# Mixture-of-experts kernel: GpSimd's gate multiplication as tensor-tensor with a repeated column

## What is computed

```python
top_v, top_i = lax.top_k(logits, TOP_K)          # TOP_K = 2 of 8 experts
gates = jax.nn.softmax(top_v, axis=-1)
...
for e in range(N_EXPERTS):
    out = out + combine[..., e:e + 1] * swiglu(h, w1[e], w3[e], w2[e])
```

## Time and profile before

| what | value |
|---|---|
| runs shown | 1646.36, 1650.67, 1651.36 us, median 1650.67 |
| span of the profiled execution, first to last instruction | 1645.5 us |
| TensorE busy in the span | 96% |
| DVE busy | 78% |
| ACT busy | 63% |
| GpSimd busy | 9% |
| mean granted TensorE clock | 0.990 |
| HBM traffic | 278 GB/s over the span |

### The profile page before, as it was taken

The page is one execution under the profiler, slowest core; times in us unless marked ns, Lnnn a source line. Parts: engine busy times, 40 slices in busy tenths (PEclk is TensorE's granted clock), DMA queues, the critical chain, the costliest instruction groups (busy, mean ns, idle before and its releaser), DMA issues.

```text
span 1645.5 us, 27766 instructions
## 1 busy us (share of the span) xinstructions
PE 1585.1 (96%) x10290; PEld 1363.3 (83%) x10290; DVE 1283.7 (78%) x1252; ACT 1041.8 (63%) x1038; POOL 139.9 (9%) x152
## 2 busy tenths in 40 slices
PE   7999989999899999899999999999999999999997
PEld 7987789999898778788888888888888888888776
DVE  4885556555558656688889889889888888988997
ACT  4634454344354445577777777777777777777675
POOL 1062000000006200100000000000000000001720
PEclk9999999999999999999999999999999999999999
DMA  7429165542252105699999999999999999999992
GB/s 252 159 89 398 55 256 184 186 170 99 80 176 88 40 2 225 247 374 375 382 375 374 389 375 377 382 374 384 378 375 361 399 373 367 395 373 369 398 356 111
DMA packets 68272, 457.56 MB, mean 278 GB/s; under 512 B 7296, under 2 KB 8480, under 8 KB 16752
## 3 DMA queue, kind: packets, MB, share of 16 engines
q1 hardware_dynamic: 59984, 425.80, 67.1%
q0 software_dynamic: 8080, 30.84, 4.9%
q10 hardware_dynamic: 144, 0.05, 0.0%
HBM read 433.07 MB, written 23.59 MB: 278 GB/s over the span
## 4 chain that ended last, share of the span: by engine, by line
PE 54%; issue 3%; DVE 3%; ACT 2%; DVEq 0%; ACTq 0%
PE bank L417 33%; PE bank L442 17%; DVE wl L495 2%; PE bank L430 1%; ACT wh L491 1%; PE bank L738 1%; PE bank L1271 1%; DVE gl L586 0%; PE bank L814 0%; PE bank L1276 0%; PE bank L483 0%; DVE gate L577 0%; ACT wide L1770 0%; ACT oh L728 0%; DVE rstd L2026 0%
## 5 line engine op out<-in xcount | busy, mean ns | idle before, releaser
L495 DVE TENSOR_TENSOR wl<-ring,wh 128x2048 fp32r<-128x2048 f32 x369 | 854.0, 2318 | 157.7 <-ACT wh L491 154.4
L491 ACT ACTIVATE wh<-ring 128x2048 fp32r<-128x2048 f32 x369 | 706.6, 1917 | 99.5 <-PE bank L442 46.9
L417 PE MATMUL bank<-wh,xh 128*128 128x512 f32 x896 | 358.0, 400 | 3.6 <-DVE wl L495 3.0
L417 PE MATMUL bank<-wh,xl 128*128 128x512 f32 x896 | 350.3, 391 | 0.0
L417 PE MATMUL bank<-wl,xh 128*128 128x512 f32 x896 | 349.6, 390 | 0.0
L417 PEld LDWEIGHTS bank<-wh,xh 128*128 128x128 f32 x896 | 168.3, 188 | 36.7 <-DVE wl L495 3.7
L417 PEld LDWEIGHTS bank<-wh,xl 128*128 128x128 f32 x896 | 168.2, 188 | 35.5
L417 PEld LDWEIGHTS bank<-wl,xh 128*128 128x128 f32 x896 | 168.7, 188 | 32.2
L442 PE MATMUL bank<-wh,gh 128*128 128x512 f32 x448 | 175.4, 392 | 6.3 <-DVE gl L586 6.3
L442 PE MATMUL bank<-wh,gl 128*128 128x512 f32 x448 | 174.4, 389 | 0.0
L442 PE MATMUL bank<-wl,gh 128*128 128x512 f32 x448 | 174.3, 389 | 0.0
(11 more groups left out here) (336 smaller groups left out, 2434.2 us busy)
## 6 DMA issues: line engine op xcount, KB each, us to landing
ring<-in_moe_w SPq DMA_DIRECT2D x336, 1024.0 KB, 5.0
ring<-in_ffn_w SPq DMA_DIRECT2D x33, 1024.0 KB, 4.8
ring<-in_w_in SPq DMA_DIRECT2D x24, 1024.0 KB, 4.9
ring<-in_w_out SPq DMA_DIRECT2D x8, 1024.0 KB, 4.8
job_x<-xrow POOLq DMA_DIRECT2D x1, 8192.0 KB, 27.3
job_y<-xrow POOLq DMA_DIRECT2D x1, 8192.0 KB, 47.7
xrow<-job_x POOLq DMA_DIRECT2D x7, 512.0 KB, 9.3
job_y<-yj POOLq DMA_DIRECT2D x7, 512.0 KB, 4.4
```

The lines of the kernel that those rows point to most:

```text
L417: ins = nc.tensor.matmul(up_bank(run, par, 0)[:], x[:, 0:C], w[b][:, k], **kw)
L491: nc.scalar.activation(wh[:, buf], flat_slot(slot), ACT.Copy).then_inc(sem("w_high"), 1)
L495: nc.vector.tensor_tensor(wl[:, buf], flat_slot(run.place(i)[0]), wh[:, buf].bitcast(F32), ALU.subtract).then_inc(sem("w_split"), 1)
```

## The change

The multiplication by one scalar per partition becomes a multiplication of two tensors, the second of which is the same gate column, repeated along the row by a step of zero. Shapes, order, waits and the additions behind it stay.

```diff
             for tt in range(TT):
                 for i in range(2):
                     y = yrow(tt, i)
-                    settle(nc.gpsimd.tensor_scalar(y, y, choice("gate")[:, i, tt:tt + 1], None, ALU.mult))
+                    settle(nc.gpsimd.tensor_tensor(y, y, choice("gate")[:, i, tt:tt + 1].broadcast_to([P, D]), ALU.mult))
                     settle(nc.gpsimd.tensor_tensor(xtok()[:, tt], xtok()[:, tt], y, ALU.add), "rows_summed")
```

## The result

The changed kernel takes 1654.7 us (median of 6 runs, 1651.3 to 1659.2), the kernel before 1647.5 beside it (median of 6, the three that were shown among them, 1646.0 to 1651.4): ratio 1.0038, 95% interval 1.0024 to 1.0052, some 6.3 us slower (4.0 to 8.6). Forecast were +7.7 us and 1658.4, range 1651 to 1662.

What follows compares the result with a forecast made beforehand. DVE was taken to bound the stretch of GpSimd's sums, TensorE the rest. Delays of 17.4 us, less 3 x 1.1 made good and 0.6 cushion, lose 13.4 against 5.7: +7.7 us, 1650.67 to 1658.4, range 1651 to 1662.

Steps and rivals of the forecast that it cites:

- So it gets in even between back-to-back subtractions.: DVE's paired subtractions: a queued GpSimd tensor-tensor starts between them too, giving three places in each DVE step.
- first rival: Last job's sums: a queued tensor-tensor gets in only at `gl` and `gate`, not inside the pair; +5.7 us, 1656.4; chance 0.19.
- A repeated operand costs the same, and I take 2.59 us.: GpSimd's new products of 128x1024: each priced like an addition with two full operands, 2.59 us.
- the 0.628 us: Duration of 256-wide GpSimd instructions with a repeated operand, used as evidence that repetition saves nothing against 0.61 us.
- The third rival: GpSimd's products: the repeated operand is fetched once, 1.06 us each; +1.7 us, 1652.4; chance 0.10.
- Delay 2.42: Inside DVE's subtraction pair: each queued GpSimd tensor-tensor delays the next `wl` by 2.42 us, at three places.
- 2.09: At `gl` and `gate` on DVE: each queued GpSimd tensor-tensor delays the next `wl` by 2.09 us, at four places.
- 17.4: DVE beside GpSimd's eight instructions: total delay in us, 1.77 + 3 x 2.42 + 4 x 2.09.
- 3.3 us made good: DVE over three steps of the stretch: recovers 1.1 us a step against TensorE's 8.42 us step.
- 0.6 of cushion: DVE's lead ahead of TensorE before the stretch: absorbs 0.6 us of the delay.
- The signs it named: Changed profile: first product 2.59 us, queued instructions about 4.6, eight `wl` of 4.1 to 4.7, three GpSimd starts per 13.9 us step.
- The rival that was built on length: Last job's sums: DVE pays by the length of GpSimd's stretch, whatever stands in it; -1.9 us, 1648.7; chance 0.06.

Runs made afterwards that it cites:

- the second trace: The changed kernel as it is, run and profiled again beside the others: ratio 1.0040 (1.0024 to 1.0057) to the kernel before.
- products by a column alone: The kernel before with the four sums left out and its tensor-scalar products kept: ratio 0.9973 (0.9958 to 0.9987).
- the sums alone: The kernel before with the four products left out, fetched rows added without their gates: ratio 1.0008 (0.9991 to 1.0026).

## Why the prediction was right, point by point

- **The cause.** Rightly placed: DVE blocked by GpSimd's tensor-tensors, in the last job alone. Ahead of it nothing but scatter moved.
- **"So it gets in even between back-to-back subtractions."** Right: the product of 1552.33 and the sum of 1564.55 delayed the second of a pair by 1.68 and 2.20 us. That step chose between forecast and first rival. Three GpSimd instructions met each DVE step (steps of 12.7 and 12.2 us for the 13.9 forecast).
- **"A repeated operand costs the same, and I take 2.59 us."** Wrong in size, the first mis-sized term. Queued product against queued sum: 3.83 against 4.33, 0.50 us less, four times: 2.0 us of delay too many. The mixer's 256-wide rows behind the 0.628 us repeat an operand only 16 and 32 at a time, not along the whole row; the rate of those didn't carry over. The third rival, one fetch, isn't it either: a copy at `gl` costs 0.49, the repeated product 1.35, the full one 1.86.
- **"Delay 2.42", "2.09".** The second: 2.20 and 1.86 for the sums. A queued instruction of this size begins some 0.34 us before the recorded end of the `wl` (the sum of 1547.93 ended at 1552.25, 2.25 us after the `wl` of 1546.10 + 3.90, where its own length is 2.59), not 0.11 as beside the mixer's smaller ones. Seven instructions are queued (the first product isn't), and seven times 0.23 is 1.6 us, the second mis-sized term. Both terms together: 17.4 - 3.6 = 13.8, measured 13.8 and, in the second trace, 13.5. That the first agrees so closely is partly luck: this trace has two delays inside a pair and not the three of the forecast, and a later start of the first product.
- **Slack.** 3.3 us made good and 0.6 of cushion would leave 13.8 - 3.9 = 9.9 of loss; 10.6 were measured, so 0.7 too much slack had been counted. The eight delayed `wl`, three to a step, are 2.7 steps and not three: an estimate of 0.4 us of it. The rest stays open. This error and the two above partly cancelled.
- **The signs it named.** Three GpSimd instructions for each DVE step and eight long `wl` came true. Too high were the first product (2.59 us, measured 1.90), the queued instructions (4.6; 3.83 and 4.32), the eight `wl` (4.1 to 4.7; four are 4.1 to 4.5 and four 3.6 to 4.0) and the length of GpSimd's stretch (35.1 us, to 1574.3; measured 31.2).
- **Sum.** +7.7 forecast; +4.7 to +4.8 of loss by the traces, +6.3 us (4.0 to 8.6) by the ratio. The forecast of 1658.4 us is 3.7 too high. The loss was put 2.9 us too high (delays 3.6 too large, less the 0.7 of slack), and the three runs shown had their median 3.2 us above that of all six (1647.5); on the other side the medians differ by 7.2 us, 2.4 more than the losses. That last part stays open; the interval reaches down to 4.0, and the place where the last job starts scatters by 5 us. So it is partly luck that the number came out as near as it did. The number alone would also have fitted the first rival (+5.7 us, 1656.4), even a little better; only the delays inside the pair tell them apart. At the upper end of the range, every queued block at 2.42 us adds 1.3 us by the prediction's own prices (four places at 0.33), not 1.7, which changes nothing here.
- **The Trainium skill's rule** (SBUF — State Buffer, "Who interferes with whom") of a port held for the whole instruction: for tensor-tensors these traces agree, since a queued one holds a `wl` back for nearly its own length. For the other forms the recorded length says little: 2.98 us for a copy that delays 0.49. Of the four products by a column alone, the two that came up inside a pair last 5.14 us and delay nothing, and the two that started ahead of a pair last 3.35 and 3.07 us and delay its first `wl` by 0.20, though they had started before it. There the traces don't agree with the rule. The rival that was built on length fell with the sums alone.
- **The Trainium skill's floor for two inputs** (GPSIMD Engine Reference, "Instruction dispatch"): between full tile and copy lie 1.37 us of block, between repeated column and copy 0.86. Two inputs do cost more than one here, with a step of zero less than with a full tile.

## What to carry to other kernels

From these runs: price a GpSimd instruction by what it withholds from DVE's two-input instructions, not by its own duration: here four products in the form that runs 17.0 us cost nothing, and in the one that runs 14.1 they cost 3.7. Beside a DVE that is nearly full prefer forms on GpSimd that read one tensor, and count how many gaps DVE leaves per step, since a queued instruction that reads two took every one here. If DVE has idle time anywhere before the result is due, four fused instructions of 1.28 us there beat eight on GpSimd: 0.9971 of before, and 0.7% below the changed kernel.

## What was not expected of the hardware

- Delay of one DVE subtraction (128x2048, two SBUF inputs) by a queued GpSimd instruction of 128x1024 float32, at `gl` or `gate` / inside the pair: copy 0.49 / 0.80 us, product by a constant 0.49 / 0.83, tensor-tensor with a repeated column 1.35 / 1.68, with two full tiles 1.86 / 2.20. Product by a column: 0.20 to 0.28 where it starts ahead of the pair, 0.49 to 0.58 on the single where DVE has no idle time, and none inside the pair.
- A tensor-scalar that reads its scalar from SBUF is passed over by DVE's next back-to-back subtraction (it lasts 5.14 us when queued 0.3 us ahead of the end of the pair's first `wl`, 6.89 when 2.1 us ahead), one with a constant is not (2.95 us).
- A tensor-tensor with a repeated column is 0.50 us shorter at 1024 elements than one with a full tile; at 256, repeated 16 and 32 at a time, no gain was seen.
